# A two-layer decoder trunk: weight blocks stored contiguously in order of use, tokens stored transposed, parameters as one table, first norm summed from transposed tokens

## The reference

```python
h = concatenate([meta, x])                                   # 528 x 2048
# layer A: xn = rmsnorm(h, a_norm)
x_m, o_pre, z = split(xn @ w_in, 3)                          # w_in 2048 x 12288
x_c = silu(causal_conv4(x_m))
q, k = x_c @ w_q, x_c @ w_k;  v = x_m @ w_v                  # per head, 512 -> 256, 256, 512
gates = [q, k, v] @ w_gate + b_gate                          # 6144 -> 16: ig, log-forget
hA = chunked mLSTM recurrence(q, k, v, gates)                # normalised by max(|den|, exp(-m))
y = (headnorm(hA * sigmoid(o_pre)) * head_norm + skip * x_c) * silu(z)
h = h + y @ w_out                                            # 4096 -> 2048
# layer B: xn = rmsnorm(h, b_norm)
q, k, v, f, z = split(xn @ w_in_b)                           # 2048 x (4*2048 + 16)
o = softmax(rmsnorm(q) rmsnorm(k)^T/sqrt(128) + cumulated log-forget, causal) v
h = h + (o * silu(z)) @ w_out_b                              # 2048 -> 2048
out = rmsnorm(h, final_norm)[16:]
```

## Time and profile before

| | us |
|---|---|
| median of 3 runs (lowest, highest) | 3151.26 (3147.39, 3153.11) |
| the profiled execution, first to last instruction (its span; no other time of it is given) | 3145.4 |
| PE busy | 3002.3 (95%) |
| DVE / ACT / POOL busy | 1363.9 / 1099.7 / 210.1 |
| moved by DMA | 342.11 MB, mean 109 GB/s |
| start until PE begins block 2 | 68.09 |
| A1 / A2 / A3 / B1 / B2, by eye from the chain | 60-690 / 690-1612 / 1612-1996 / 1996-2923 / 2923-3145 |

### The profile page before, as it was taken

The page is one execution under the profiler, slowest core; times in us unless marked ns, Lnnn a source line. Parts: engine busy times, 40 slices in busy tenths (PEclk is TensorE's granted clock), DMA queues, the critical chain, the costliest instruction groups (busy, mean ns, idle before and its releaser), DMA issues.

```text
span 3145.4 us, 52249 instructions
## 1 busy us (share of the span) xinstructions
PE 3002.3 (95%) x21904; PEld 2851.2 (91%) x21904; DVE 1363.9 (43%) x1739; ACT 1099.7 (35%) x1426; POOL 210.1 (7%) x235
## 2 busy tenths in 40 slices
PE   6999999999999999999999999899899998999897
PEld 6999999999999999999999999798789988889786
DVE  5555555554544444444442332534344443344432
ACT  5444444443332232332231222334334343343422
POOL 0000000000010000000000022100000000000121
PEclk9999999999999999999999999999999999999999
DMA  5333333344433433433453232354343354343332
GB/s 189 127 121 123 121 122 122 123 141 121 125 117 106 121 116 114 127 115 106 133 205 100 80 93 82 116 94 62 80 93 75 87 75 60 92 84 87 122 93 80
DMA packets 469863, 342.11 MB, mean 109 GB/s; under 512 B 15283, under 2 KB 451781, under 8 KB 462437
## 3 DMA queue, kind: packets, MB, share of 16 engines
q1 hardware_dynamic: 453808, 244.99, 31.3%
q0 software_dynamic: 15488, 95.24, 8.1%
q10 hardware_dynamic: 452, 0.14, 0.0%
HBM read 292.82 MB, written 47.52 MB: 108 GB/s over the span
## 4 chain that ended last, share of the span: by engine, by line
PE 88%; DMA 5%; DVE 3%; ACT 2%; issue 2%; SPq 0%; ACTq 0%; POOL 0%; DVEq 0%; POOLq 0%; PEldq 0%
PE mm L1443 73%; PE ax L1443 6%; DMA w_raw<-in_b_w_in_dram 4%; PE ax L1597 3%; PE ax L1650 3%; DVE w_lo L955 1%; PE mm L1538 1%; PE ax L1753 1%; ACT w_hi L562 1%; DVE xl L967 0%; PE mm L1476 0%; DVE vn L1058 0%; PE ax L1806 0%; PE ax L1574 0%; DMA x_nat<-in_x_dram 0%
## 5 line engine op out<-in xcount | busy, mean ns | idle before, releaser
L1443 PE MATMUL mm<-xh,w_hi 128*128 128x264 f32 (+1 forms) x5920 | 1370.0, 302 | 43.8 <-DVE xl L967 22.5
L1443 PE MATMUL mm<-xl,w_hi 128*128 128x264 f32 (+1 forms) x5920 | 1360.7, 301 | 0.0
L1443 PE MATMUL mm<-xh,w_lo 128*128 128x264 f32 (+1 forms) x5920 | 1357.8, 300 | 0.0
L1443 PEld LDWEIGHTS mm<-xh,w_hi 128*128 128x128 f32 x5920 | 954.7, 190 | 85.5 <-issue 33.6
L1443 PEld LDWEIGHTS mm<-xh,w_lo 128*128 128x128 f32 x5920 | 949.4, 190 | 33.2
L1443 PEld LDWEIGHTS mm<-xl,w_hi 128*128 128x128 f32 x5920 | 950.3, 190 | 31.4
L955 DVE TENSOR_TENSOR w_lo<-w_raw,w_hi 128x2048 fp32r<-128x2048 f32 x225 | 515.4, 2291 | 614.9 <-ACT w_hi L562 614.9
L562 ACT ACTIVATE w_hi<-w_raw 128x2048 fp32r<-128x2048 f32 x225 | 430.8, 1915 | 551.2 <-PE mm L1443 442.4
L1244 DVE TENSOR_TENSOR h<-h,mm 128x528 f32 (+1 forms) x32 | 22.5, 705 | 229.6 <-PE mm L1443 224.7
L486 POOL TENSOR_TENSOR rtmp<-rtmp,sq 128x528 f32<-128x528 f32 (+1 forms) x32 | 85.4, 2668 | 457.8 <-ACT sq L795 329.0
L725 ACT ACTIVATE ot<-mm 128x528 f32<-128x528 f32 x32 | 19.5, 611 | 236.9 <-PE mm L1443 227.2
(11 more groups left out here) (262 smaller groups left out, 2949.2 us busy)
## 6 DMA issues: line engine op xcount, KB each, us to landing
w_raw<-in_a_w_in_dram SPq DMA_DIRECT2D x96, 1024.0 KB, 5.9
w_raw<-in_b_w_in_dram SPq DMA_DIRECT2D x65, 1024.0 KB, 15.5
w_raw<-in_a_w_out_dram SPq DMA_DIRECT2D x32, 1024.0 KB, 6.0
w_raw<-in_b_w_out_dram SPq DMA_DIRECT2D x16, 1024.0 KB, 5.9
xc_scratch<-xc POOLq DMA_DIRECT2D x32, 264.0 KB, 5.7
qk_scratch<-qkv POOLq DMA_DIRECT2D x8, 1056.0 KB, 4.2
qk_whole<-qk_scratch POOLq DMA_DIRECT2D x8, 1056.0 KB, 5.4
xc_load<-xc_scratch POOLq DMA_DIRECT2D x8, 1056.0 KB, 5.7
```

The costliest lines, as they stand in the source:

```text
L1443: i = pe.matmul(ps[:, at:at + n], w, v[:, t0:t0 + n], start=first and k == 0, stop=last and k == 2)
```

## The change

- Six arrays take the place of 21. `weights` holds all 225 blocks, each 128 x 2048 numbers in one piece, in order of use, so each partition's share of a block is one run of 8192 bytes. q and k of a head are one block. `gate_weights` is the same for w_gate, one load per head instead of three. `params` is all parameter vectors, already transposed, as one 128x274 table. `xt` is meta tokens and tokens, transposed, as 128 x 16 x 528.
- The start loads `xt` in four parts straight into `hT0`. The transpositions, copies out of PSUM, diagonals, the store to `h_d` and the waits for it are gone. ACT squares the 16 transposed tiles, DVE adds them up (15 additions), PE sums over the partitions with ones (`full_sum`), ACT makes Ln and Exp of the 128x528 result. Block 0 is rounded between the squares and Ln. Blocks 0 and 1 run as `two_blocks`, as in layer B.
- A3 reads h from `xt` instead of `h_d`. The weight loads of SP are loops over the block number. The separate wait between the loads of w_k and w_q is gone.

```diff
-            def load(b, par_, src, cols=P, tiles=KT, at=0, done=None):
+            def load(b, par_):
                 if not (isinstance(b, int) and b < 2):
                     sp.wait_ge(w_lo_ready, b - 1)
-                full = w_raw[par_][:, :].rearrange("p (k m) -> p k m", k=tiles)
-                sp.dma_start(full[:, :, at:at + cols], src).then_inc(done or w_raw_ready[par_], 16)
+                sp.dma_start(w_raw[par_][:, :],
+                             weights[ds(b, 1)].rearrange("a p n -> (a p) n")).then_inc(w_raw_ready[par_], 16)
...
-            sp.dma_start(meta_nat[:, :], meta_tokens).then_inc(meta_loaded, 16)
-            for i in range(NT):
-                if i == NT // 2:
-                    load_xm(0, 0)
-                sp.dma_start(x_nat[:, i, :], x[0, i * P:(i + 1) * P, :]).then_inc(x_loaded[i], 16)
-            for c in range(1, CT):
-                load_xm(0, c)
+            for i in range(X_PARTS):
+                w = KT // X_PARTS
+                sp.dma_start(flat(hT0[:, i * w:(i + 1) * w, :]), flat(xt[:, i * w:(i + 1) * w, :])).then_inc(x_loaded[i], 16)
+            for c in range(CT):
+                load(c, c % 2)
             sp.wait_ge(xl_ready, KT)
-            sp.wait_ge(h_stored, 16 * H_PARTS)
...
-            load(B1_0, B1_0 % 2, w_in_b[:, :, 3 * BH * BD:3 * BH * BD + P])
-            with sp.Fori(0, BH) as h:
-                for k in range(B1_PER):
-                    part = (0, BH * BD, 2 * BH * BD, Z_B)[k]
-                    load(h * B1_PER + (B1_0 + 1 + k), (B1_0 + 1 + k) % 2, w_in_b[:, :, ds(h * BD + part, P)])
+            with sp.Fori(0, (BLOCKS - O0_BLOCK - 4) // 2) as i:
+                for k in range(2):
+                    load(i * 2 + (O0_BLOCK + 4 + k), k)
...
-            for i in range(H_PARTS):
-                w = KT // H_PARTS
-                pool.wait_ge(h_copied, (i + 1) * w)
-                pool.dma_start(h_d[:, i * w * T:(i + 1) * w * T],
-                               flat(hT0[:, i * w:(i + 1) * w, :])).then_inc(h_stored, 16)
...
-            pool.dma_start(flat(hT3[:, :, :]), h_d).then_inc(h_loaded, 16)
+            pool.dma_start(flat(hT3[:, :, :]), flat(xt[:, :, :])).then_inc(h_loaded, 16)
...
+            act.dma_start(par[:, :], params).then_inc(par_loaded, 16)
...
-            for i in range(NT):
-                if i == NT // 2:
-                    round_w(0, 0)
-                act.wait_ge(x_loaded[i], 16)
-                act.activation(flat(hT0[:, :, :])[:, i * D:(i + 1) * D], x_nat[:, i, :], ACT.Square,
-                               accum_out=stat0[:, 0, i:i + 1]).then_inc(stat0_ready, 1)
...
+            for j in range(KT):
+                act.wait_ge(x_loaded[j * X_PARTS // KT], 16)
+                if j >= 2:
+                    act.wait_ge(sum0_ready, j - 1)
+                act.activation(sq[j % 2][:, :], hT0[:, j, :], ACT.Square).then_inc(sq0_ready, 1)
+            round_w(0, 0)
+            act.wait_ge(sumsq0_done, 1)
+            inv_sqrt(halves(ax[0]), rstd[:, :], 1.0 / D, sq[0][:, :], 1, two, ln0_ready, rstd0_ready)
             round_w(1, 1)
             for j in range(KT):
                 act.wait_ge(xt_ready, j + 1)
                 act.activation(XH[:, j, :], xt0[j % 2][:, :], ACT.Copy).then_inc(xh_ready, 1)
-                if j + 2 < KT:
-                    copy_h(j + 2)
             act.wait_ge(xl_ready, KT)
-            act.wait_ge(h_stored, 16 * H_PARTS)
...
+            for j in range(1, KT):
+                dve.wait_ge(sq0_ready, j + 1)
+                if j > 1:
+                    dve.wait_ge(sum0_ready, j)
+                dve.tensor_tensor(rtmp[:, :], sq[0][:, :] if j == 1 else rtmp[:, :], sq[j % 2][:, :],
+                                  ALU.add).then_inc(sum0_ready, 2 if j == 1 else 1)
             low_w(0, 0)
...
-                if j == 2:
+                if j == 4:
                     low_w(1, 1)
...
+            pe.wait_ge(sum0_ready, KT)
+            full_sum(ax[0], rtmp, HT).then_inc(sumsq0_done, 1)
+            two_blocks(0, 0, (mm[0], mm[1]), (ALL, ALL), 0)
...
+    blocks = _blocks(a_in, d, [c * p for c in range(ct)])
+    for h in range(1, ah):
+        cols = [h * dv + c * p for c in range(ct)]
+        blocks += _blocks(a_in, d, cols[:1]) + qkv(h - 1) + _blocks(a_in, d, cols[1:])
...
+    blocks += _blocks(b_in, d, [3 * bh * bd])
+    for h in range(bh):
+        blocks += _blocks(b_in, d, [h * bd, (bh + h) * bd, (2 * bh + h) * bd, 3 * bh * bd + bh + h * bd])
```

More of the change, by code:

```diff
@@ L14, with hybrid_trunk @@
 BANK = 512
-def hybrid_trunk(nc, x, meta_tokens, a_norm, a_w_in, a_conv_w, a_conv_b, a_w_q, a_w_k, a_w_v,
-                 a_w_gate, a_b_gate, a_head_norm, a_skip, a_w_out, b_norm, b_w_in, b_b_f,
-                 b_q_norm, b_k_norm, b_w_out, final_norm, out):
-    _, SEQ, D = x.shape
-    META = meta_tokens.shape[0]
+def hybrid_trunk(nc, xt, weights, gate_weights, params, a_b_gate, b_b_f, sizes, out):
+    SEQ, META, D, AI, AH, DV, DQK, NG, BH, BD, TAPS = sizes
     T = META + SEQ
@@ L47, in hybrid_trunk @@
     W_AFTER = 5
-    H_PARTS = 4
+    X_PARTS = 4
     EPS = 1e-6
@@ L355, in load_head_a1 @@
             def load_head_a1(h):
-                load_xm(h, 0)
-                load_qkv(h - 1, 1)
-                for c in range(1, CT):
-                    load_xm(h, c)
-            def load_a2(h, k, b):
-                part = (1 + k // CT) * AI + k % CT * P
-                load(b, k % 2, w_in_a[:, :, ds(h * DV + part, P)])
+                b0 = xm_block(h, 0)
+                for k in range(3):
+                    load(b0 + k, k % 2)
+                load_gate_weights(h - 1)
+                for k in range(3, A1_PER):
+                    load(b0 + k, k % 2)
@@ L593, in _ @@
-            act.wait_ge(stat0_ready, NT + 1)
-            for r, c0, c1 in ((P, 0, NT), (META, NT, NT + 1)):
-                act.activation(stat0[0:r, 1, c0:c1], stat0[0:r, 0, c0:c1], ACT.Ln, bias=eps_t[0:r, 0:1],
-                               scale=1.0 / D).then_inc(stat0_ready, 1)
-            act.wait_ge(stat0_ready, NT + 3)
-            for r, c0, c1 in ((P, 0, NT), (META, NT, NT + 1)):
-                act.activation(stat0[0:r, 2, c0:c1], stat0[0:r, 1, c0:c1], ACT.Exp, scale=-0.5).then_inc(stat0_ready, 1)
@@ L664, in _ @@
                 conv_tile(0, c, c + 2, c % 2)
-            act.wait_ge(par_loaded, 16 * 11)
+            act.wait_ge(par_loaded, 16 * 3)
             def head_a1(h):
@@ L1879, in _, with _blocks, _pack, qkv @@
             i.then_inc(sumsq_done, 1)
-_INS = ['x', 'meta_tokens', 'a_norm', 'a_w_in', 'a_conv_w', 'a_conv_b', 'a_w_q', 'a_w_k', 'a_w_v', 'a_w_gate',
-        'a_b_gate', 'a_head_norm', 'a_skip', 'a_w_out', 'b_norm', 'b_w_in', 'b_b_f', 'b_q_norm', 'b_k_norm',
-        'b_w_out', 'final_norm']
+def _blocks(w, rows, starts):
+    p = 128
+    t = w.reshape(rows // p, p, w.shape[1])
+    return [t[:, :, s:s + p].transpose(1, 0, 2).reshape(p, rows) for s in starts]
+def _pack(np, i):
+    p = 128
+    a_in, b_in = i["a_w_in"][0], i["b_w_in"][0]
+    d = a_in.shape[0]
+    ai = a_in.shape[1] // 3
+    ah, dv, dqk = i["a_w_q"].shape[1:]
+    ng = i["a_w_gate"].shape[2]
+    bh, bd = i["b_b_f"].shape[1], i["b_q_norm"].shape[1]
+    ct = dv // p
+    tokens = np.concatenate([i["meta_tokens"], i["x"][0]], axis=0)
+    xt = np.ascontiguousarray(tokens.T.reshape(d // p, p, tokens.shape[0]).transpose(1, 0, 2))
+    def qkv(h):
+        qk = np.concatenate([i["a_w_q"][0, h], i["a_w_k"][0, h]], axis=1)
+        return [m.reshape(ct, p, 2 * dqk).transpose(1, 0, 2).reshape(p, ct * 2 * dqk) for m in (qk, i["a_w_v"][0, h])]
+    blocks = _blocks(a_in, d, [c * p for c in range(ct)])
+    for h in range(1, ah):
+        cols = [h * dv + c * p for c in range(ct)]
+        blocks += _blocks(a_in, d, cols[:1]) + qkv(h - 1) + _blocks(a_in, d, cols[1:])
+    gates = [h * dv + (1 + k // ct) * ai + k % ct * p for h in range(ah) for k in range(2 * ct)]
+    blocks += _blocks(a_in, d, gates[:1]) + qkv(ah - 1) + _blocks(a_in, d, gates[1:])
+    for f in range(ai // d):
+        blocks += _blocks(i["a_w_out"][0][f * d:(f + 1) * d], d, range(0, d, p))
+    blocks += _blocks(b_in, d, [3 * bh * bd])
+    for h in range(bh):
+        blocks += _blocks(b_in, d, [h * bd, (bh + h) * bd, (2 * bh + h) * bd, 3 * bh * bd + bh + h * bd])
+    blocks += _blocks(i["b_w_out"][0], bh * bd, range(0, d, p))
+    wg = i["a_w_gate"][0].reshape(-1, p, ng)
+    qt = dqk // p
+    tiles = [list(range(h * qt, (h + 1) * qt)) + list(range((ah + h) * qt, (ah + h + 1) * qt))
+             + list(range(2 * ah * qt + h * ct, 2 * ah * qt + (h + 1) * ct)) for h in range(ah)]
+    gate_weights = np.stack([wg[t].transpose(1, 0, 2).reshape(p, len(t) * ng) for t in tiles])
+    vectors = [*i["a_conv_w"][0], i["a_conv_b"][0], i["a_head_norm"][0], i["a_skip"][0], i["a_norm"][0],
+               i["b_norm"][0], i["final_norm"], i["b_q_norm"][0], i["b_k_norm"][0]]
+    params = np.concatenate([v.reshape(-1, p) for v in vectors], axis=0)
```

(4 more changed lines are left out.)

144 lines of the change are left out of this document (24 added, 120 removed).

## The result

| | before | after |
|---|---|---|
| median (lowest, highest), four runs each on one chip | 3149.32 (3144.98, 3153.11) | 3100.06 (3099.22, 3101.12) |
| the profiled execution: its span | 3145.4 | 3097.7 |
| the same execution's time | not given | 3099.22 |
| block 2 begins | 68.09 | 59.95 |
| A2, by eye from PE's rows | 689.1 to 1618.3 | 682.1 to 1601.1 |

The ratio is 0.9844 [0.9829, 0.9858]: 49 us less.

A forecast was written before the change was run, and what follows sets the result against it. PE was taken as the limit, busy 3002.3 of 3145.4 us. B1's loads 29.8 plus the start 8.7 gave 38.5 us less, a span of 3106.9; with 5.9 added, 3113 us, range 3105 to 3123.

The forecast's parts named there:

- B1's slow loads, 29.8 us: In B1, slow b_w_in loads delay PE in two clusters of heads; contiguous blocks gain all 29.8 us, bounds 28 to 31.
- The rival that the loads outlive the layout: In B1, something other than layout slows the loads, so only the start gains: 3142.6 us, chance 0.07; in part 3128, 0.04.
- Contiguous loads are no slower than 19.3 us: In the A stages, a load may take 19.3 us before costing time; rival of slow contiguous loads has chance 0.03.
- The start, 8.7 us: From launch to block 2: it begins at 59.4 instead of 68.1 us, gaining 8.7, bounds 5 to 12.
- the rival on the clock: At the start, PE stays at its lower clock through the pairs, block 2 at 68.8: 3122 us, chance 0.07.
- In the other stages the load is hidden already, so a quicker one is worth 0 there: Outside B1, quicker or merged weight loads gain 0 us as long as loads keep under 19.3 us.
- part 3, 0 each: Parameter table, A3's read of h from `xt` and fewer SP instructions: 0 us each, beside PE's work of A1 and A3.
- a better case: Waits held for PE's own shrink too, as 16 times fewer packets share DMA engines with POOL's transfers: 3100 us, chance 0.04.
- Median = span + 5.9: Whole kernel: the median of the runs is 5.9 us above the profiled span, kept for the forecast: 3106.9 to 3112.8 us.

The follow-up runs named there:

- before_padded: The kernel before the change with only the rows of b_w_in padded from 32,832 to 33,024 bytes; 3120.84 us, ratio 0.9912 to the kernel before.
- pad83: The kernel after the change with 83 small transpositions put into PE's program ahead of its first real work; 3106.81 us, ratio 0.9864 to the kernel before.

## Why the prediction was off

By its own steps:

- **B1's slow loads, 29.8 us.** Right: 29.9 in the trace, 29.6 by `before_padded`. The way it was read, the period of the same block from head to head against undisturbed heads, gave the size to a tenth. The rival that the loads outlive the layout is dead. But the reason given, runs of 8192 bytes in place of 512, was not it: runs of 512 bytes at any other pitch tried do as well.
- **Contiguous loads are no slower than 19.3 us.** Right: 4.9 at the median.
- **The start, 8.7 us.** 8.1 measured. Single terms were off and cancelled in part: the tokens came at 415 instead of 358 GB/s, but the additions took 0.81 and not 0.75 and so became what sets the sum, 20.5 against 19.2; PE's sum took 2.10 and not 1.2, after 20 us of idleness, but its end at 22.72 is only 0.04 behind that of the table load (22.68), which had to wait for the rounding of block 0 (to 21.38 and not 20.4, since the squares followed the slower additions); rstd 25.4 against 24.3; first `xl` 27.8 against 26.9; block 0's evacuation 53.4 against 52.8; block 2 59.95 against 59.4. PE's rows stayed at 0.64 to 37.9, where PE was paced by DVE's 1.42 us a tile; it was back at 2.4 GHz ahead of the pairs, so the rival on the clock did not come about.
- **"In the other stages the load is hidden already, so a quicker one is worth 0 there", and part 3, 0 each. This is the step that failed.** A2 gained 10.1 us. The loads were indeed hidden; what was not are the pauses of PE's program at each turn of A2's loop. They stood in the trace of before as waits for "issue", 15.6 us in six places, and I had left them out, because nothing in the diff touches that loop. But the diff takes 83 matmuls out of PE's program ahead of it, and the length of that program is worth 6.7 us (`pad83`; 8.1 in the loop of the traces). I had counted those matmuls as work in time that the start had anyway, and not as program. What else the DMA engines carry may add a few us; the traces don't settle how many. The rival "a better case", to which I gave 0.04, named 3100 and waits held for PE's own, but not their cause: its picture of packets in POOL's way was wrong, and most of the gain came from the program's length and not from the traffic. That its number came out is luck.
- **Median = span + 5.9.** Wrong: the execution after lasted 3099.22 with a span of 3097.7, 1.5 outside it, and every other execution has 1.2 to 1.7. So the execution profiled before was one of the short ones, near 3147, and the choice of it was luck. That error is 4.4 us, about a third of the miss. Of the miss of 13.6 against the profiled execution, 9.2 is the span (A2 +10.1, B1's first blocks +1.2, B1 +0.1, the start -0.6, the turn to A2 -1.1, A3 -0.5) and 4.4 this.

What stays open: why a pitch of 32,768 + 64 bytes with 512-byte runs is slow at addresses 4096 bytes apart, while 32,768 + 128 is not; why the same slow heads cost 30 us in one program and 64 to 68 in two others; and why some pauses have a stretch at 1.2 GHz behind them and others not.

## What to carry to other kernels

When one array's loads are slow while others of the same size are not, change its row pitch by 64 or 192 bytes before laying everything out anew; and don't take the loss in one program as its price, since the same layout cost 30, 75 and 81 us. Read each "wait for issue" of the limiting engine as well, whatever the diff touches: a long loop of its program can stop at every turn, and a change of the program ahead of the loop can shorten or lengthen that. Take the median from the spans of several executions, not from one.

## What the hardware showed that I had not expected

- 1 MB in 2048 runs of 512 bytes: 5.8 to 6.0 us at pitches of 8,192, 49,152, 49,216, 33,024 and 32,896 bytes, but 15.5 to 19.4 at the median and up to 44 at 32,832. A packet took 0.178 against 0.031 us. Slow places are 4096 bytes apart and move with the address, one execution each.
- PE stops 1.3 to 2.8 us at each jump back of a loop of 902 matmuls a turn, though its data are ready, and not at those of loops with 628 or 347; written out, it does not stop. A 16 KB packet of its program comes in each stop, and the stop is longer where another was fetched just before. Behind some stops the clock is at 1.2 GHz for 3.4 us or 6.8, which costs 1.7 us or more, by estimate half of the stretch.
- A chain of dependent additions of 128 x 528 on DVE takes 0.81 us each, 0.71 of it the addition.
